# One expert-output copy a chunk earlier, warm-up products around the first gather, and head work moved between VectorE and GpSimd

## Chip, cores and metric

The kernel runs on one core of one Trainium2 chip. The metric is the device time of one execution in microseconds (us), lower is better. Float32 arithmetic is emulated on TensorE: each product of two float32 matrices is computed as three products of "high" and "low" parts in the fp32r format.

## What is computed

Two transformer blocks in a row over 256 tokens of width 1024. The first block has two layers with a second stream of 256 context tokens beside the tokens `x`; each layer norms both streams, projects them (`h @ w_in`), norms the query and key heads, rotates the heads of `x` by position (rope), attends, mixes, and runs a SwiGLU. The second block has an even layer (differential attention, a Mamba scan, SwiGLU) and an odd layer (sparse attention "nsa", latent attention "mla", then a mixture of 8 experts with two chosen per token). What the change touches, cut from the reference:

```python
qa, ka = apply_rope(qa, cos, sin), apply_rope(ka, cos, sin)      # x heads, first block
qc, kc = apply_rope(qc, cos, sin), apply_rope(kc, cos, sin)
qac = rms_norm(qac, q_norm)                                      # context heads, no rope
...
q = apply_rope(rms_norm(q, nsa_q_gain), cos, sin)                # odd layer, 8 heads of 64
...
logits = t @ router
top_val, top_idx = lax.top_k(logits, 2)
for e in range(8):
    out = out + gates[:, e:e + 1] * swiglu(t, w_gate[e], w_up[e], w_down[e])
```

## The kernel before

The program is a row of blocks; between two blocks all engines meet. Within a block each engine has its own instruction list, written out by hand, and executes it in that order; semaphores connect them. SP's queue issues the weight loads into a ring of four slots (`load_stream`, and the `sync` list of `moe`).

**A weight chunk's way.** In `linear`, `ffn` and `moe` a piece of weights (128x1024 float32) lands in the ring; ScalarE copies it to its high part `w_hi` (L978 in `linear`, L1188 in `ffn`, L3335 and L3340 in `moe`), VectorE subtracts that from the piece to get `w_lo` (L1066, L1262, L3407), TensorE multiplies (L880 to L882: high by high, low by high, high by low). Only three buffer pairs exist in `linear`, so the split of piece q waits until TensorE is through with piece q-3.

**Linear over the context (first block).** `linear` starts with a front: TensorE turns the normed rows, ScalarE makes `src_hi` (L690), VectorE `src_lo` (L646), eight tiles of 128x256. VectorE's order is: `w_lo` of piece 0, `src_lo` tiles 0 to 3, `w_lo` of piece 1, `src_lo` tiles 4 to 7, `w_lo` 2, `w_lo` 3, and so on. Piece 1 multiplies tiles 2 and 3, piece 2 tiles 4 and 5. Beside this GpSimd runs `x_turns1` (L1485): `rope_rows` (L529; L537 to L540) of the first eight heads of `x`, then the root of the context heads' mean squares (`rsqrts`, L494, the power on L500), for which it waits for VectorE, then `rope_rows` of the second eight heads. The context heads are squared, summed, scaled and multiplied with their gain on VectorE (`ctx_heads1`, L1496) after chunk 1 and chunk 2. This block runs twice: with 6 chunks in layer 0, where other small weight loads ("riders") are interleaved on the same SP queue, and with 3 chunks in layer 1.

**Linear of the odd layer.** Seven chunks. GpSimd runs `nsa_heads` (L2255): after the first eviction it norms eight query heads alone (`norm_rows`, L503, with squares on L510, five halving additions on L514, the power on L518, scale L523, gain L526), then waits for VectorE's mean squares of the keys and takes their root (L500), then ropes the queries. VectorE runs `nsa_keys` (L2270): squares of two key pairs after chunk 3, then key 0 after chunk 4 and key 1 after chunk 5 (scale L1462, gain L1469, rope L537 to L540). The last evictions (L1095) are of chunks 5 and 6. After its last product TensorE runs warm-up products (`tail=14`).

**The experts.** `moe` (L3122) walks through jobs b (8 in this trace), each of `FC` = 22 steps r. At step r TensorE does `up` of chunk r (12 products of 512 columns), on even steps it turns the activation of the pair before (L3249), and on odd steps it does `down` of two earlier chunks (L3249's result, split into `act_hi`, L3353, and `act_lo`, L3428). So a job's last two downs happen at step 1 of the next job. The job's output in banks 0 and 1 is then copied: `keep_output` on ScalarE (`y_hi`, L3324, two halves, and the turned pick matrix, L3326) and `keep_output_rest` on VectorE (`y_lo`, L3398). Both are called at step 3: ScalarE's behind that step's weight splits and `act_hi`, VectorE's behind the splits of gate and up but ahead of those of down and of `act_lo`. TensorE's `down` at step 3 writes the same banks and waits for `y_kept`.

Before the walk, `moe` makes the first pick matrices on VectorE (L3377), TensorE gathers the tokens in four parts (L3218), ScalarE and VectorE split them (L3315, L3384), and then the first weights are split. `keep_warm(p, pe, bank, n)` (L262) issues n products of 128 columns on TensorE whose result nobody reads.

Of the kernel before, what the change touches and what calls it, by code (L numbers as in the profile page):

```python
# [23 lines left out]
NT = T // P  # L24
D = 1024
KT = D // P
HD = 64
# [466 lines left out]
def rsqrts(p, pool, widths, parts=P, first=0):  # L494

    for w in widths:
        p.roots += 1
        pool.wait_ge(p.meansq.sem, p.roots)
        v = p.small[0:parts, first:first + w]
        pool.tensor_tensor(v, v, p.neg_half[0:parts, 0:w], ALU.pow).then_inc(p.rstd.sem, 1)  # L500
# [984 lines left out]
def x_turns1(p, proj, queries):  # L1485

    def beside(pool, taken):
        for a in (0, 896):
            rope_rows(pool_chain(p, pool), pool, heads_of(proj, a, 8), p.con_at(CON1, "rope_c", NT),
                      p.con_at(CON1, "rope_s", NT), p.big[:, 0:2048])  # L1490
            if a == 0:
                rsqrts(p, pool, [16 if queries else 4])
    return beside


# [759 lines left out]
def nsa_heads(p):  # L2255

    def beside(pool, taken):
        chain, junk = pool_chain(p, pool), p.big[:, 0:2048]
        pool.wait_ge(*taken(1))
        v = heads_of(p.proj, 0, 8)  # L2260
        norm_rows(p, chain, pool, v, [(0, 8, p.row(ROWS2, "nsa_q"))], junk, True)
        rsqrts(p, pool, [8])
        rope_rows(chain, pool, v, p.con_at(CON2, "rope_c", NT), p.con_at(CON2, "rope_s", NT), junk)
    return beside


# [3 lines left out]
def nsa_keys(p):  # L2270

    keys = [heads_of(p.proj, 768 + 256 * w, 2) for w in range(2)]
    st = p.small[:, 0:8]

    def inline(dve, chain, c):
        if c == 3:
            for w in range(2):
                square_sums(p, chain, dve, keys[w], p.work[:, 0:256], st[:, 4 * w:4 * w + 4])
            mean_squares(p, dve, st, HD)
        if c == 4:  # L2280
            rsqrt(p, dve, st)
        if c in (4, 5):
            for w in (c - 4,):
                scale_heads(chain, dve, keys[w], st[:, 4 * w:4 * w + 4])
                gain_heads(chain, dve, keys[w], p.row(ROWS2, "nsa_k", 1 + w, HD))
                rope_rows(chain, dve, keys[w], p.con_at(CON2, "rope_c", NT), p.con_at(CON2, "rope_s", NT), p.work[:, 512:1024])
    return inline
# [834 lines left out]
def moe(p):  # L3122
# [63 lines left out]
    with nc.Block(no_gpsimd_drain=True) as block:  # L3186
# [20 lines left out]
        def _(pe):  # L3207
# [69 lines left out]
            def step(i, b, r, first, last):  # L3277
# [21 lines left out]
                if r == FC + 2:  # L3299
                    turn_weights(i, b)  # L3300
                    for q in range(4):
                        scatter(i, b, q)

            for part in range(4):
                gather(0, 0, part)
            walk(pe, between, step)

        @block.scalar
        def _(act):
            between = act.value_load(p.trip[0:1, 1:2], min_val=1, max_val=3)  # L3310

            def keep_job(i, j, part):

                act.wait_ge(*job_at(gathered, i, 2, 2 * j + part + 1))
                act.activation(sources[j // 2 % 2][0][:, 2 * part:2 * part + 2, :].rearrange("p k s -> p (k s)"),  # L3315
                               p.ps[G_BANK[part]][:, :], ACT.Copy).then_inc(job_hi.sem, 1)

            def keep_output(i, j):

                act.wait_ge(*at(p.w_used[DOWN], i, (j + 1) * FC))  # L3320
                if not (isinstance(i, int) and j == 0):
                    act.wait_ge(*job_at(scattered, i, 4, 4 * j))
                for hf in range(2):
                    act.activation(yH[:, hf * 512:hf * 512 + 512], p.ps[hf][:, :], ACT.Copy).then_inc(y_hi.sem, 1)  # L3324
                act.wait_ge(*job_at(wt_turned, i, 1, j + 1))
                act.activation(WT, p.ps[5][:, 0:T], ACT.Copy).then_inc(wt_kept.sem, 1)  # L3326

            def step(i, b, r, first, last):
                k = b * FC + r

                def hi_side(half):
                    if half == 0:
                        act.wait_ge(*loaded_at(p.slot_loaded, g0, i, k))
                    act.wait_ge(*at(p.w_used[half], i, k - 1))
                    act.activation(sets[k % 2][0][:, half, :], side_piece(k, half), ACT.Copy).then_inc(p.w_hi[half].sem, 1)  # L3335

                def hi_down(m):
                    act.wait_ge(*loaded_at(p.dn_loaded, 0, i, m))
                    act.wait_ge(*at(p.w_used[DOWN], i, m - 1))
                    act.activation(sets[m % 2][0][:, DOWN, :], down_piece(m), ACT.Copy).then_inc(p.w_hi[DOWN].sem, 1)  # L3340

                if r < FC:
                    hi_side(0)
                    hi_side(1)
                c = k // 2 - 1
                if r % 2 == 0 and there(r, 2, first):
                    act.wait_ge(*at(p.w_used[1], i, 2 * c + 2))
                    act.activation(th[:, c % 2, :], p.ps[2 + c % 2][:, 0:T], ACT.Tanh, scale=0.5).then_inc(th_ready.sem, 1)
                if r % 2 and there(r, 3, first):
                    hi_down(k - 3)  # L3350
                    act.wait_ge(*pair_at(a_turned, i, c + 1))
                    act.wait_ge(*at(p.w_used[DOWN], i, 2 * c))
                    act.activation(p.actH[:, :], p.ps[4][:, 0:T], ACT.Copy).then_inc(act_hi.sem, 1)  # L3353
                    hi_down(k - 2)
                if r == 3 and not first:
                    keep_output(i, b - 1)
                if r - 3 in GATHER_AT and b % 2 and not last:
                    keep_job(i, b + 1, GATHER_AT.index(r - 3))
                if r == FC + 2:
                    keep_output(i, b)  # L3360

            for part in range(4):
                keep_job(0, 0, part)
            walk(act, between, step)

        @block.vector
        def _(dve):
# [33 lines left out]
            def step(i, b, r, first, last):  # L3401
                k = b * FC + r

                def lo(m, piece, kind):
                    wh, wl = [v[:, kind, :] for v in sets[m % 2]]
                    dve.wait_ge(*at(p.w_hi[kind], i, m + 1))
                    dve.tensor_tensor(wl, piece, wh.bitcast(F32), ALU.subtract).then_inc(p.w_lo[kind].sem, 1)  # L3407

                if r < FC:
                    lo(k, side_piece(k, 0), 0)  # L3410
                    lo(k, side_piece(k, 1), 1)
                if r == 3 and not first:
                    keep_output_rest(i, b - 1)
                c = k // 2 - 1
                bank = p.ps[2 + c % 2]
                if r % 2 == 0 and there(r, 2, first):
                    dve.wait_ge(*pair_at(th_ready, i, c + 1))
                    dve.scalar_tensor_tensor(out=zz[:, c % 2, :], in0=th[:, c % 2, :], scalar=1.0, in1=bank[:, 0:T],
                                             op0=ALU.add, op1=ALU.mult).then_inc(half_ready.sem, 1)
                    dve.wait_ge(*pair_at(half_ready, i, c + 1))  # L3420
                    if not (first and r < 6):
                        dve.wait_ge(*pair_at(a_turned, i, c - 1))
                    dve.scalar_tensor_tensor(out=aJ[:, c % 2, :], in0=zz[:, c % 2, :], scalar=0.5, in1=bank[:, T:2 * T],
                                             op0=ALU.mult, op1=ALU.mult).then_inc(a_ready.sem, 1)
                if r % 2 and there(r, 3, first):
                    lo(k - 3, down_piece(k - 3), DOWN)
                    dve.wait_ge(*pair_at(act_hi, i, c + 1))
                    dve.tensor_tensor(p.actL[:, :], p.ps[4][:, 0:T], p.actH[:, :].bitcast(F32),  # L3428
                                      ALU.subtract).then_inc(act_ready.sem, 1)
                    lo(k - 2, down_piece(k - 2), DOWN)  # L3430
                if r - 3 in SCATTER_AT and not first:
                    add_scattered(i, b - 1, SCATTER_AT.index(r - 3))
                if r == 6 and b % 2 and not last:
                    dve.wait_ge(*job_at(wt_turned, i, 1, b))
                    make_pick(i, b + 1)
                if r - 4 in GATHER_AT and b % 2 and not last:
                    keep_rest(i, b + 1, GATHER_AT.index(r - 4))
                if r == FC + 2:
                    keep_output_rest(i, b)
                    for q in range(4):  # L3440
                        add_scattered(i, b, q)
# [195 lines left out]
```

## Time and profile before

| what | value |
|---|---|
| median of 3 runs | 2532.47 us (2528.02 to 2534.73) |
| the profiled execution's own time | 2531.21 us |
| span of the profiled execution | 2529.0 us |
| TensorE busy | 2367.0 us, 94% |
| VectorE busy | 1764.6 us, 70% |
| ScalarE busy | 1262.2 us, 50% |
| GpSimd busy | 186.8 us, 7% |
| moved by DMA | 542.42 MB, mean 214 GB/s |

Names in the profile: PE is TensorE's matrix product, PEld its weight load, DVE is VectorE, ACT ScalarE, POOL GpSimd, SP the queue that issues loads. A row of a timeline gives start, duration, engine, line, operation, output and inputs, the count of merged instructions, and in brackets how long the engine had been idle and what ended that. The TensorE clock column is the granted clock as a share of 2.4 GHz. "PEq" of a line means the engine sequencer, in practice the meeting of all engines between two blocks. A start and a duration are on the engine: an instruction that is held up by something shows a longer duration.

### The profile page before, as it was taken

Reading aid. Unit: us, or ns where it says so; the run is one execution under the profiler, and the core shown is the slowest. Engines: PE = TensorE matmul, PEld = TensorE weight load, DVE = VectorE, ACT = ScalarE, POOL = GpSimd, SP = SyncE. Lnnn points to the kernel's source line nnn. Section 1 sums busy time; section 2 is a strip of 40 time slices with the busy share of each in tenths; the row PEclk is TensorE's granted clock in tenths of the full one; section 3 lists DMA queues with packets and bytes.
Section 4 is the critical chain, followed back from the end, with each engine's and each line's share of the span. In section 5 each row is a group of like instructions: output and inputs, shape, how many; then the busy total and the mean of one; then the engine's idle time right before and its main releaser. Section 6 shows DMA issues by size and latency. Waiting matters only on the chain. (4 is left out here: it accounts for less than half of the span.)

```text
span 2529.0 us, 37705 instructions
## 1 busy us (share of the span) xinstructions
PE 2367.0 (94%) x14147; PEld 1996.9 (79%) x14147; DVE 1764.6 (70%) x2539; ACT 1262.2 (50%) x1891; POOL 186.8 (7%) x168
## 2 busy tenths in 40 slices
PE   7889999999998999999799998879999999999998
PEld 6677689889986779988689987567787877877876
DVE  3555565565567565567765567558999999998997
ACT  2245244344443544442444442336777777776775
POOL 0310000000005000008100013000000000000000
PEclk9889999999999999999999997799999999999999
DMA  8520565646644055534045551027998988998995
GB/s 322 232 105 34 200 241 221 230 175 225 222 154 150 1 189 191 184 133 163 1 169 181 187 209 43 1 92 299 352 352 323 370 343 332 360 338 334 352 346 220
DMA packets 82199, 542.42 MB, mean 214 GB/s; under 512 B 9328, under 2 KB 9840, under 8 KB 33904
## 3 DMA queue, kind: packets, MB, share of 16 engines
q1 hardware_dynamic: 79184, 529.57, 56.2%
q10 hardware_dynamic: 2848, 10.55, 1.1%
q8 instruction: 114, 1.87, 0.3%
q14 instruction: 53, 0.43, 0.1%
HBM read 539.03 MB, written 1.05 MB: 214 GB/s over the span
## 5 line engine op out<-in xcount | busy, mean ns | idle before, releaser
L3407 DVE TENSOR_TENSOR w_lo<-ring,w_hi 128x1024 fp32r<-128x1024 f32 x528 | 617.8, 1219 | 28.2 <-ACT w_hi L3340 25.4
L880 PE MATMUL bank<-w_hi,src_hi 128*128 128x512 f32 (+1 forms) x1184 | 477.3, 403 | 20.8 <-DVE src_lo L646 12.7
L881 PE MATMUL bank<-w_lo,src_hi 128*128 128x512 f32 (+1 forms) x1184 | 464.9, 393 | 0.0
L882 PE MATMUL bank<-w_hi,src_lo 128*128 128x512 f32 (+1 forms) x1184 | 464.3, 392 | 0.0
L880 PE MATMUL bank<-src_hi,w_hi 128*128 128x256 f32 x1472 | 422.9, 287 | 7.9 <-DVE src_lo L646 7.3
L1188 ACT ACTIVATE w_hi<-ring 128x1024 fp32r<-128x1024 f32 x260 | 274.2, 1057 | 297.4 <-PE bank L882 273.2
L1262 DVE TENSOR_TENSOR w_lo<-ring,w_hi 128x1024 fp32r<-128x1024 f32 x260 | 317.9, 1223 | 146.9 <-ACT w_hi L1188 146.3
L881 PE MATMUL bank<-src_lo,w_hi 128*128 128x256 f32 x1472 | 417.2, 283 | 0.0
L882 PE MATMUL bank<-src_hi,w_lo 128*128 128x256 f32 x1472 | 417.1, 283 | 0.0
L3335 ACT ACTIVATE w_hi<-ring 128x1024 fp32r<-128x1024 f32 x352 | 352.5, 1055 | 2.0 <-PE bank L882 2.0
L880 PEld LDWEIGHTS bank<-src_hi,w_hi 128*128 128x128 f32 x1472 | 282.6, 192 | 21.0 <-issue 15.7
L880 PEld LDWEIGHTS bank<-w_hi,src_hi 128*128 128x128 f32 x1184 | 225.0, 190 | 78.8 <-issue 29.1
L880 PE MATMUL bank<-w_hi,act_hi 128*128 128x512 f32 x688 | 271.9, 395 | 15.2 <-DVE act_lo L3428 15.2
L881 PEld LDWEIGHTS bank<-src_lo,w_hi 128*128 128x128 f32 x1472 | 282.9, 192 | 2.3 <-issue 0.7
L882 PEld LDWEIGHTS bank<-src_hi,w_lo 128*128 128x128 f32 x1472 | 282.9, 192 | 0.0
L881 PE MATMUL bank<-w_lo,act_hi 128*128 128x512 f32 x688 | 271.2, 394 | 0.0
L882 PE MATMUL bank<-w_hi,act_lo 128*128 128x512 f32 x688 | 270.1, 393 | 0.0
L882 PEld LDWEIGHTS bank<-w_hi,src_lo 128*128 128x128 f32 x1184 | 224.9, 190 | 50.4
L881 PEld LDWEIGHTS bank<-w_lo,src_hi 128*128 128x128 f32 x1184 | 225.7, 191 | 44.4 <-issue 0.7
L978 ACT ACTIVATE w_hi<-ring 128x1024 fp32r<-128x1024 f32 x120 | 126.5, 1060 | 228.8 <-PE bank L882 145.4
L1066 DVE TENSOR_TENSOR w_lo<-ring,w_hi 128x1024 fp32r<-128x1024 f32 x120 | 171.9, 1439 | 84.1 <-ACT w_hi L978 83.6
L3340 ACT ACTIVATE w_hi<-ring 128x1024 fp32r<-128x1024 f32 x176 | 185.3, 1053 | 2.9 <-PE bank L882 2.9
(439 smaller groups left out, 2771.0 us busy)
## 6 DMA issues: line engine op xcount, KB each, us to landing
ring<-in_moe SPq DMA_DIRECT2D x176, 1024.0 KB, 6.7
ring<-in_ffn SPq DMA_DIRECT2D x66, 1536.0 KB, 6.7
ring<-in_moe SPq DMA_DIRECT2D x176, 512.0 KB, 5.7
ring<-in_ffn_ev SPq DMA_DIRECT2D x22, 1536.0 KB, 6.6
oT<-in_w_ada SPq DMA_DIRECT2D x20, 1024.0 KB, 6.9
big<-in_w_ada SPq DMA_DIRECT2D x20, 1024.0 KB, 8.4
ring<-in_w_in SPq DMA_DIRECT2D x18, 1024.0 KB, 7.9
ring<-in_w_out SPq DMA_DIRECT2D x12, 1024.0 KB, 9.9
```

The costliest lines, as they stand in the source:

```text
L880: pe.matmul(out, ah, bh, start=start and i == 0, stop=False, skip_group_check=True)
L881: pe.matmul(out, ah, bl, start=False, stop=False, skip_group_check=True)
L882: mm = pe.matmul(out, al, bh, start=False, stop=stop and i == n - 1, skip_group_check=True)
L978: act.activation(p.wH[:, b, :], p.ring[:, g % RING, (q % 2) * PIECE:(q % 2 + 1) * PIECE], ACT.Copy).then_inc(p.w_hi[b].sem, 1)
L1066: ins = dve.tensor_tensor(p.wL[:, b, :], p.ring[:, g % RING, (q % 2) * PIECE:(q % 2 + 1) * PIECE], p.wH[:, b, :].bitcast(F32), ALU.subtract)
L1188: act.activation(p.wH[:, kind, :], piece(c, kind), ACT.Copy).then_inc(p.w_hi[kind].sem, 1)
L1262: dve.tensor_tensor(p.wL[:, kind, :], piece(c, kind), p.wH[:, kind, :].bitcast(F32), ALU.subtract).then_inc(p.w_lo[kind].sem, 1)
L3335: act.activation(sets[k % 2][0][:, half, :], side_piece(k, half), ACT.Copy).then_inc(p.w_hi[half].sem, 1)
L3340: act.activation(sets[m % 2][0][:, DOWN, :], down_piece(m), ACT.Copy).then_inc(p.w_hi[DOWN].sem, 1)
L3407: dve.tensor_tensor(wl, piece, wh.bitcast(F32), ALU.subtract).then_inc(p.w_lo[kind].sem, 1)
```

## The change

Four edits; no arithmetic of the result changes, only where and when it is done.

1. `moe`: `keep_output` and `keep_output_rest` are called at step 2 in place of step 3. On ScalarE the call stands behind step 2's tanh; on VectorE it stands behind step 2's two activation operations.
2. `moe`: ten warm-up products before the first gather and ten after it.
3. `x_turns1` (both context linears): GpSimd ropes both groups of eight heads first and takes the context's root afterwards.
4. Odd layer's linear: the squares, sums and mean squares of the eight query heads go from GpSimd to VectorE (after chunk 1); GpSimd takes the root (now over 16 values by `rsqrts`), scales, applies gain and rope, and takes the keys' root last. VectorE turns key 0 after chunk 5 and key 1 after chunk 6, in place of after 4 and 5.

```diff
@@ x_turns1
         for a in (0, 896):
             rope_rows(pool_chain(p, pool), pool, heads_of(proj, a, 8), p.con_at(CON1, "rope_c", NT),
                       p.con_at(CON1, "rope_s", NT), p.big[:, 0:2048])
-            if a == 0:
-                rsqrts(p, pool, [16 if queries else 4])
+        rsqrts(p, pool, [16 if queries else 4])
@@ nsa_heads
-        pool.wait_ge(*taken(1))
         v = heads_of(p.proj, 0, 8)
-        norm_rows(p, chain, pool, v, [(0, 8, p.row(ROWS2, "nsa_q"))], junk, True)
+        st = p.small[:, 224:240]
+        rsqrts(p, pool, [16], first=224)
+        pool.wait_ge(p.rstd.sem, p.roots)
+        scale_heads(chain, pool, v, st)
+        gain_heads(chain, pool, v, p.row(ROWS2, "nsa_q"))
+        rope_rows(chain, pool, v, p.con_at(CON2, "rope_c", NT), p.con_at(CON2, "rope_s", NT), junk)
         rsqrts(p, pool, [8])
-        rope_rows(chain, pool, v, p.con_at(CON2, "rope_c", NT), p.con_at(CON2, "rope_s", NT), junk)
@@ nsa_keys, inline(dve, chain, c)
+        if c == 1:
+            square_sums(p, chain, dve, heads_of(p.proj, 0, 8), p.work[:, 0:1024], p.small[:, 224:240])
+            mean_squares(p, dve, p.small[:, 224:240], HD)
+            p.meansq.passed(1)
+            p.rstd.passed(1)
...
-        if c == 4:
+        if c == 5:
             rsqrt(p, dve, st)
-        if c in (4, 5):
-            for w in (c - 4,):
+        if c in (5, 6):
+            for w in (c - 5,):
@@ moe, TensorE
+            keep_warm(p, pe, p.ps[4], 10)
             for part in range(4):
                 gather(0, 0, part)
+            keep_warm(p, pe, p.ps[4], 10)
             walk(pe, between, step)
@@ moe, ScalarE, step
-                if r == 3 and not first:
+                if r == 2 and not first:
                     keep_output(i, b - 1)
@@ moe, VectorE, step
                     lo(k, side_piece(k, 1), 1)
-                if r == 3 and not first:
-                    keep_output_rest(i, b - 1)
...
                     dve.scalar_tensor_tensor(out=aJ[:, c % 2, :], in0=zz[:, c % 2, :], scalar=0.5, in1=bank[:, T:2 * T],
                                              op0=ALU.mult, op1=ALU.mult).then_inc(a_ready.sem, 1)
+                if r == 2 and not first:
+                    keep_output_rest(i, b - 1)
```

## Rows read from the trace of the kernel before

**Rows 1.** Busy time by stretch: from, to, length, engines, granted clock, DMA.

```profile
1717.00:2529.00 812.00, 787.80 (x3520) 637.25 (x3520) 742.15 (x863) 575.05 (x738) 0.00 (x0) 0.99 0.89 337
```

**Rows 2.** Waits, TensorE, 1725 to 2510 us: waiter, releaser, total, times, longest.

```profile
PE bank L880 <- DVE act_lo L3428: 14.0, 7, 2.2
```

**Rows 3.** Timeline of TensorE at one change of job (steps 1 to 3).

```profile
1818.12 0.39 PE L882 MATMUL bank<-w_hi,act_lo 128*128 128x512 f32 x1
...
1821.48 0.48 PE L880 MATMUL bank<-w_hi,src_hi 128*128 128x512 f32 x1
...
1826.47 0.47 PE L880 MATMUL bank<-w_hi,act_hi 128*128 128x512 f32 x1 [1.93 <-DVE act_lo L3428]
```

**Rows 4.** Timeline of ScalarE at the same change of job.

```profile
1816.36 2.00 ACT L3335 ACTIVATE w_hi<-ring 128x1024 fp32r<-128x1024 f32 x2
...
1822.99 1.07 ACT L3324 ACTIVATE y_hi<-bank 128x512 fp32r<-128x512 f32 x2
...
1824.21 2.02 ACT L3335 ACTIVATE w_hi<-ring 128x1024 fp32r<-128x1024 f32 x2
```

**Rows 5.** Timeline of VectorE at the same change of job.

```profile
1818.54 2.35 DVE L3407 TENSOR_TENSOR w_lo<-ring,w_hi 128x1024 fp32r<-128x1024 f32 x2
1823.61 1.29 DVE L3398 TENSOR_TENSOR y_lo<-bank,y_hi 128x512 fp32r<-128x512 f32 x2 [2.72 <-ACT y_hi L3324]
```

**Rows 6.** Timeline of TensorE from the router to the first expert.

```profile
1700.73 3.37 PE L265 MATMUL bank<-ident 128*128 128x128 f32 x28
1707.24 0.58 PE L3218 MATMUL bank<-pick,xn_hi 128*128 128x256 f32 x1 [3.14 <-DVE pick L3377]
...
1713.76 0.28 PE L3218 MATMUL bank<-pick,xn_lo 128*128 128x256 f32 x1
1717.02 0.76 PE L880 MATMUL bank<-w_hi,src_hi 128*128 128x512 f32 x1 [2.98 <-DVE w_lo L3407]
```

**Rows 7.** Busy time and granted clock (third figure from the end) by microsecond, there.

```profile
1706.00:1707.00 1.00, 0.00 (x0) 0.00 (x0) 0.69 (x4) 0.00 (x0) 0.00 (x0) 0.80 0.00 0
...
1720.00:1721.00 1.00, 1.00 (x5) 0.77 (x5) 0.28 (x1) 0.99 (x1) 0.00 (x0) 0.88 0.79 311
```

**Rows 8.** Front of layer 1's context linear, timelines of GpSimd, VectorE, TensorE.

```profile
798.82 2.45 POOL L540 TENSOR_TENSOR proj<-big 128x1024 f32<-128x1024 f32 x1
...
797.03 5.19 DVE L646 TENSOR_TENSOR src_lo<-work,src_hi 128x256 fp32r<-128x256 f32 x4
...
803.50 1.43 DVE L646 TENSOR_TENSOR src_lo<-work,src_hi 128x256 fp32r<-128x256 f32 x4
804.85 2.35 DVE L1066 TENSOR_TENSOR w_lo<-ring,w_hi 128x1024 fp32r<-128x1024 f32 x2
...
806.26 0.40 PE L880 MATMUL bank<-w_hi,src_hi 128*128 128x512 f32 x1
```

**Rows 9.** End of that linear, timelines of VectorE and TensorE.

```profile
820.72 2.48 DVE L1469 TENSOR_TENSOR projc<-projc,rows 128x256 f32<-128x256 f32 x1
...
823.80 0.66 PE L1593 MATMUL bank<-ident,projc 128*128 128x128 f32 x2 [5.78 <-PEq L954]
```

**Rows 10.** Layer 0's context linear, timelines of ScalarE and TensorE.

```profile
125.53 2.01 ACT L978 ACTIVATE w_hi<-ring 128x1024 fp32r<-128x1024 f32 x2 [9.70 <-DMA ring<-in_w_in]
...
131.78 1.05 PE L339 MATMUL bank<-small,rows 128*128 128x2 f32 x8 [3.76 <-DVE rows L331]
...
142.02 1.07 PE L323 MATMUL bank<-oT,rows 128*32 128x256 f32 x16 [2.02 <-DVE mod L349]
```

**Rows 11.** Odd layer's linear, timelines of GpSimd, VectorE, TensorE.

```profile
1509.08 5.97 POOL L514 TENSOR_TENSOR big<-big 128x512 f32<-128x512 f32 x5
...
1515.71 2.91 POOL L518 TENSOR_TENSOR small<-small,neg_half 128x16 f32<-128x16 f32 x1
...
1515.89 1.22 DVE L1066 TENSOR_TENSOR w_lo<-ring,w_hi 128x1024 fp32r<-128x1024 f32 x1 [1.35 <-ACT w_hi L978]
...
1541.84 1.94 PE L2371 MATMUL bank<-ident,proj 128*128 128x128 f32 x8 [5.33 <-PEq L954]
```

## The prediction

> **What bounds the kernel now.** I read the page's busy shares first, then the stretch of the experts, then who waits there, then the timelines of single places. TensorE is busy 2367.0 of 2529.0 us, 94%, so only its gaps and its slow-clock stretches can be won. The experts take 812 us, TensorE busy for 787.8 of them and VectorE for 742.2 [rows 1]: TensorE leads, VectorE has about a tenth to spare. The list of waits shows that TensorE stops there almost only at the seven changes of job: 14.0 us in 7 waits on `act_lo`, 2.0 each [rows 2]. The rest of the change lies in three linears and at the start of the experts, where VectorE and GpSimd decide.
>
> **Part 1, output copied at step 2.** Before, TensorE ends step 3's `up` and cannot go on with `down` until 1826.47 [rows 3]: `act_lo` stands on VectorE behind `y_lo`, and VectorE sat idle 2.72 us for `y_hi`, which ScalarE started only at 1822.99 [rows 4, 5]. Afterwards ScalarE reaches the copy with nothing else to do but to wait for the job's last `down`. That ends at 1818.12 + 0.39 = 1818.5 [rows 3]. From the start of `y_hi` to the next weight split it takes 1824.21 - 1822.99 = 1.22 [rows 4]. So step 3's first weight split, which ran at 1816.36, starts at 1819.8, 3.4 us later, and is queued behind this wait; it is done at 1820.8, the second at 1821.8, the `down` split at 1822.9, `act_hi` at about 1823.2. VectorE does `y_lo` in 1.29 by 1820.5, then step 3's first `w_lo` from 1820.9 to 1822.1 (1.17 each, half of 2.35 [rows 5]). TensorE wants it at 1821.48 [rows 3]: a new wait of 0.65. The rest of VectorE's list ends with `act_lo` at about 1824.9, and `up` ends at 1825.1. `down` starts there in place of 1826.47: 1.4 us won. Seven changes of job: **-9.8 us**. The unknown is how much of the 3.4 us on ScalarE reaches TensorE; ends: none (the whole 2.0 is won, -14) and all (3.4 - 2.0 = 1.4 lost each, +10). I take the value worked out from the lead that the rows show: `w_lo` was done at 1819.7, 1.8 ahead of its use. ScalarE and VectorE are back at their old times or earlier from step 4 on, so nothing is late next. SP's loads wait for `w_lo`, which moves by at most 2.4 us, and no engine waited for a load in the experts.
>
> **Part 2, warm-up products.** Fourteen such calls left 28 records in 3.37 us [rows 6], so ten cost 2.4 us at full clock. TensorE is idle 3.14 us before the gather and 2.98 before the first `up` [rows 6]; the second ten fit in that gap, the first ten overrun it by about 1.4 us (the block starts about 1 us before the gather does). What they may give: the gather ran from 1707.24 to 1714.0, 6.8 us at the 1.2 GHz level; the mean grant of 0.80 in the microsecond from 1706 puts the first fall at 1706.6; at the first `up` the clock was low again, until about 1720.2 (0.88 in that microsecond) [rows 7]. At 2.4 GHz the 32 gather products would take some 3.8 us, and the 3.2 us of low clock before 1720.2 would give back some 1.4. If the first ten come in time: +1.4 - 3.0 = -1.6 for the gather (the splits follow it), and -1.4 for the first `up`: -2.9. If the clock has fallen when they start, they cost about 4.5 us themselves, the gather ends later by up to 2.5, and only the second saving stands: +1. The start of the block and the fall of the clock are within 0.3 us of each other, so I take the middle: **-1.5 us**.
>
> **Part 3, both ropes first.** Two sides. At the end: in layer 1 the second rope holds VectorE's last gain for 2.48 us where the same form needs 0.43 elsewhere, and the block ends at 823.8 after a TensorE gap of 5.78 [rows 9]. Without it VectorE's last three operations end 3.4 us earlier. In layer 0 it stands behind the two TensorE gaps of [rows 10], 3.76 and 2.02.
>
> At the front: the second rope now starts at 801.3, in the stretch where TensorE waits for VectorE operation by operation. The rows show what a rope does there. While GpSimd's last two rope operations ran (until 801.27), four `src_lo` took 5.19 us; the next four, with GpSimd silent, took 1.43 [rows 8]. The starts and ends fit strict turns: one VectorE operation, one GpSimd operation. Going on in turns, the four operations of the second rope (about 1.15, 1.15, 2.25 and 2.2 of their own) push `src_lo` 2 to 4.5, `w_lo` 1 by 4.7 and `w_lo` 2 by 6.7 us. TensorE had started on that piece at 806.26, 0.1 us after `w_lo` was ready [rows 8]: no slack. So TensorE is 6.5 us late by then. Layer 1: +6.5 - 3.4 = **+3**. Its ends: -3.4 (front free) and +6 (the new gap also brings the clock down once). Layer 0: the same +6.7 at the front, and it is passed on, since SP issues the last weight chunks behind the riders, which wait for TensorE, and ScalarE waited for that chunk until 125.53 [rows 10]. Against it the gaps of 3.76 and 2.0 shrink by some 3.9, and the slow clock after each (about 1.6 us a time) may go. **+1**, ends -3.9 and +6.
>
> **Part 4, odd layer's linear.** GpSimd loses the squares and additions: 1.9 + 6.0 (five additions 5.97 [rows 11]). VectorE gains a square and a reduction of 128x1024, each taken at the 1.22 of an operation of that size [rows 11], and a small one, after chunk 1, where it was waiting for ScalarE; `w_lo` of the next piece comes 0.3 us later, three ahead of its use. GpSimd ends at about 1531 and not 1536, so the keys' operations on VectorE, held there as the gain was in [rows 9], are free: a whole key then takes 2.2. VectorE's tail behind TensorE's last product (about 1533.8, 0.8 later than before since `w_lo` 12 and 13 now meet the rope): eviction 0.76, key 1 in 2.2, end 1537.4 in place of 1541.3: -3.9. TensorE's gap of 5.33 at 1541.84 [rows 11] shrinks to 0.8, so the next block may begin at full clock: -1. **-5**, ends -1 and -9 (the fast clock holds on through the small products).
>
> A row and a page differ here. The power over 16 values ran from 1515.71 to 1518.62, and a `w_lo` that began 0.2 us into it took its plain 1.22 [rows 11]. The Trainium skill, "SBUF — State Buffer", Who interferes with whom, says that a VectorE instruction with two SBUF inputs and a GpSimd instruction that reads SBUF exclude one another for the whole instruction. For the ropes the trace agrees (5.19 against 1.43); for the power it doesn't, and I go by the row.
>
> **Sum.** -9.8 - 1.5 + 3 + 1 - 5 = -12.3. Against the profiled execution's own 2531.2 this gives 2518.9; the median of the runs is 1.3 higher, so 2520.
>
> **Rivals.**
> 1. *The front takes no harm* (VectorE gets in between, or the pieces have lead I don't see). Then part 3 gives -3.4 - 3.9 in place of +4: 2520 - 11.3 = 2508.7. For it: VectorE is only 70% busy. Against: 5.19 against 1.43. Chance 0.08.
> 2. *The stall at the change of job only changes its name*: `w_lo` of step 3 or of `down` comes late by 2.0 and takes the place of `act_lo`. Part 1 is 0: 2530. For it: ScalarE's 3.4 us delay is larger than the 2.0 won. Against: the lead of 1.8. Chance 0.10.
> 3. *Slower: ScalarE's in-order wait for the last `down` reaches TensorE whole.* Place: step 3's first `up`, seven times. Price 3.4 - 2.0 = 1.4 each, +9.8 in place of -9.8: 2539.6. It decides once the delay that reaches TensorE is over 2.0, that is if the lead of 1.8 is really below 0.4 after VectorE's own delay of 2.4. Chance 0.05.
> 4. *The power holds VectorE too*: in the odd layer it would now start near 1511.7, hold `w_lo` 8 until 1514.6, done 1515.8, where TensorE wants it at 1514.8: +1, 2521. That is what the page's rule gives. Chance 0.10.
>
> **Numbers.** The forecast has 0.67; its own range, with the ends above partly taken, is 2513 to 2526. The measurement tells 0.3% (7.6 us) from no change, so faster means below 2524.9. Faster: 0.62 of the forecast, 0.08, 0.09 of rival 4: 0.79. Same: 0.05, 0.10, 0.01, 0.01: 0.17. Slower: 0.04 of rival 3. The range goes from 2510 to 2529, leaving out rival 1, rival 3 and part of rival 2.
>
> **What would show it.** Part 1: at each change of job `y_hi` starts 0.1 us after the last `down`; TensorE waits about 0.65 us for `w_lo` and `down` starts 1.4 earlier. No such wait and 2.0 won would make me too cautious; one of 2 us or more makes rival 2 or 3. Part 2: gather in under 4.5 us, and 0.23 us apart from the first `up` on. Part 3: six or more us of TensorE gaps within the first ten of both context linears, none at the end. A front without them makes the prediction wrong by 11 us. Part 4: GpSimd's rope ends before 1532, and the next block starts near 1538 on the old scale.

## The result, and the profile after

The changed kernel takes 2512.66 us in the median of 5 runs (2507.91 to 2520.87), against 2532.47 before (also the median of five, where the table above has three): 19.8 us less, ratio 0.993 with an interval of 0.9911 to 0.995. The forecast was 2520 with 2510 to 2529. The profiled execution took 2507.91 us with a span of 2506.1, 22.9 less than that of before; it is 4.8 us below its own median and that of before 1.3 below, so about 3 us of these 22.9 are luck.

The table cuts both spans at the starts of blocks (first instruction of GpSimd or TensorE in them; "experts" begins at the first `up`). In brackets: us at the 1.2 GHz level, worked out from the granted clock. "nsa, mla and output linear" is called the nsa and mla block below.

| stretch, us | before | after | difference |
|---|---|---|---|
| up to layer 0's context linear | 92.6 (14.2) | 91.3 (10.8) | -1.3 |
| that linear | 61.2 (13.4) | 60.9 (13.2) | -0.3 |
| from there to layer 1's | 639.1 (24.7) | 639.4 (25.0) | +0.3 |
| layer 1's context linear | 30.8 (10.4) | 33.9 (15.9) | +3.1 |
| attention behind it | 90.6 (9.0) | 87.6 (0.0) | -3.0 |
| to the root in the odd linear's front | 573.0 (10.2) | 571.7 (10.2) | -1.3 |
| odd layer's linear from there | 54.4 (2.5) | 51.7 (0.0) | -2.7 |
| nsa, mla and output linear | 151.9 (62.4) | 149.1 (54.6) | -2.8 |
| router and gather | 23.3 (7.0) | 23.0 (3.4) | -0.3 |
| experts | 812.0 (13.3) | 797.4 (8.9) | -14.6 |

The waits of TensorE from 1712 to 2480 us, the experts: waiter, releaser, total, times, longest. It answers to [rows 2].

```profile
PE bank L880 <- DVE w_lo L3416: 3.6, 7, 0.5
```

The 14.0 us on `act_lo` are gone; seven waits of 0.5 on step 3's first `w_lo` have come, where 0.65 was forecast. One change of job in the timelines of TensorE, ScalarE and VectorE, beside [rows 3 to 5]:

```profile
1812.34 0.50 PE L880 MATMUL bank<-w_hi,src_hi 128*128 128x512 f32 x1 [0.44 <-DVE w_lo L3416]
...
1808.73 1.09 ACT L3333 ACTIVATE y_hi<-bank 128x512 fp32r<-128x512 f32 x2 [2.08 <-PE bank L882]
...
1809.96 2.02 ACT L3344 ACTIVATE w_hi<-ring 128x1024 fp32r<-128x1024 f32 x2
...
1809.36 1.29 DVE L3407 TENSOR_TENSOR y_lo<-bank,y_hi 128x512 fp32r<-128x512 f32 x2 [0.57 <-ACT y_hi L3333]
1811.06 3.50 DVE L3416 TENSOR_TENSOR w_lo<-ring,w_hi 128x1024 fp32r<-128x1024 f32 x3 [0.41 <-ACT w_hi L3344]
```

ScalarE idles 2.08 us for the last `down`, and the step's weight splits stand behind that. The front of layer 1's context linear, in the timelines of GpSimd, VectorE and TensorE, beside [rows 8, 9]:

```profile
802.80 2.52 POOL L539 TENSOR_TENSOR big<-proj,con 128x1024 f32<-128x1024 f32 x1
805.40 3.25 POOL L540 TENSOR_TENSOR proj<-big 128x1024 f32<-128x1024 f32 x1
...
795.74 7.38 DVE L646 TENSOR_TENSOR src_lo<-work,src_hi 128x256 fp32r<-128x256 f32 x4
803.04 3.35 DVE L1066 TENSOR_TENSOR w_lo<-ring,w_hi 128x1024 fp32r<-128x1024 f32 x1
806.55 3.39 DVE L646 TENSOR_TENSOR src_lo<-work,src_hi 128x256 fp32r<-128x256 f32 x4
...
824.53 0.42 DVE L1469 TENSOR_TENSOR projc<-projc,rows 128x256 f32<-128x256 f32 x1
...
806.46 0.79 PE L880 MATMUL bank<-w_hi,src_hi 128*128 128x512 f32 x1 [4.27 <-DVE w_lo L1066]
...
825.55 0.41 PE L1592 MATMUL bank<-ident,projc 128*128 128x128 f32 x2 [2.40 <-PEq L954]
```

Four `src_lo` now take 7.38 us (5.19 before) and the next `w_lo` 3.35 in place of 1.21: the two engines take turns until the second rope is over. TensorE waits 4.27 us for that `w_lo`, and starts piece 1 at the low clock (0.79 for the product behind the gap, where the one at 1812.34 above has 0.50 at full clock). At the end the gain runs at its own 0.42 (2.48 in [rows 9]), and the gap before the next block has shrunk from 5.78 to 2.40.

The odd layer's linear, timelines of GpSimd, VectorE and TensorE, beside [rows 11]:

```profile
1509.28 3.81 POOL L500 TENSOR_TENSOR small<-small,neg_half 128x16 f32<-128x16 f32 x1 [23.72 <-DVE small L1456]
...
1509.11 1.22 DVE L1066 TENSOR_TENSOR w_lo<-ring,w_hi 128x1024 fp32r<-128x1024 f32 x1
1510.58 1.23 DVE L1066 TENSOR_TENSOR w_lo<-ring,w_hi 128x1024 fp32r<-128x1024 f32 x1 [0.26 <-ACT w_hi L978]
...
1522.87 1.77 DVE L1456 TENSOR_SCALAR small<-small 128x8 f32<-128x8 f32 x1
1524.55 4.57 DVE L1066 TENSOR_TENSOR w_lo<-ring,w_hi 128x1024 fp32r<-128x1024 f32 x2
...
1525.82 0.39 PE L880 MATMUL bank<-w_hi,src_hi 128*128 128x256 f32 x1 [2.36 <-DVE w_lo L1066]
...
1536.55 1.06 PE L2378 MATMUL bank<-ident,proj 128*128 128x128 f32 x8 [0.74 <-PEq L954]
```

The gap before the next block is 0.74 and not 5.33. But the rope now meets the last two pieces, and TensorE waits 2.36 us for `w_lo` 12.

The start of the experts, timeline of TensorE, beside [rows 6]:

```profile
1697.86 4.13 PE L265 MATMUL bank<-ident 128*128 128x128 f32 x20 [1.85 <-PEq L3047]
...
1705.56 2.39 PE L265 MATMUL bank<-ident 128*128 128x128 f32 x20
1708.70 0.47 PE L880 MATMUL bank<-w_hi,src_hi 128*128 128x512 f32 x1 [0.75 <-DVE w_lo L3416]
```

The first ten warm-up calls take 4.13 us: the clock falls 0.6 us after they start, at 1698.44, and is back at 1701.85. The second ten run at full clock and take 2.39.

### The profile page after: what moved, and what is told of

It is laid out like the page before. It is cut to its first block and busy times, and to the rows that moved or that the text cites. A ratio compares the mean times of both kernels' runs of the same rounds, so it can differ in the third digit from the quotient of the medians.

```text
span 2506.1 us, 37778 instructions
## 1 busy us (share of the span) xinstructions
PE 2359.8 (94%) x14187; PEld 1993.8 (80%) x14187; DVE 1766.1 (70%) x2542; ACT 1261.8 (50%) x1891; POOL 181.5 (7%) x160
## 5 line engine op out<-in xcount | busy, mean ns | idle before, releaser
L3416 DVE TENSOR_TENSOR w_lo<-ring,w_hi 128x1024 fp32r<-128x1024 f32 x528 | 616.8, 1218 | 29.5 <-ACT w_hi L3349 24.7
L880 PE MATMUL bank<-w_hi,src_hi 128*128 128x512 f32 (+1 forms) x1184 | 478.0, 404 | 32.0 <-DVE src_lo L646 12.7
## 6 DMA issues: line engine op xcount, KB each, us to landing
ring<-in_w_out SPq DMA_DIRECT2D x12, 1024.0 KB, 10.5
```

Source lines behind the costliest of these rows:

```text
L880: pe.matmul(out, ah, bh, start=start and i == 0, stop=False, skip_group_check=True)
```

## The experiments

Each part of the change was first undone alone. The experiments ran on three chips, each beside the kernel before (median 2528.42 us for the first four, 2531.92 for the next four, 2529.41 for the last three). So whole times are compared by their ratio to it, which is 0.993 for the changed kernel; 0.001 is 2.5 us.

**The copy back at step 3.**

```diff
-                if r == 2 and not first:
+                if r == 3 and not first:
                     keep_output(i, b - 1)
```

(and VectorE's part likewise)

> The changed kernel with the output copied at step 3 again, as before. My theory: the waits of 0.5 us on the first w_lo at each change of job become waits of 2.0 us on act_lo, seven times, +10.4 us between the first up and the end; and with waits of 2 us the low clock stretches of about 3.4 us that the kernel before had at 1928 and 2331 us come back in some of them (1 to 2 us lost each), so +11 to +14 in all, 2524 to 2527 us against the changed kernel's 2512.7. Rival (the clock has nothing to do with the waits at the changes of job): no low clock between the first up and the last job, and +10.4 alone. Rival 2 (the gain in the experts was not from the copy): under +5.

Measured: 2527.21 us median (2517.8 to 2546.16), ratio to before 1.0001 (0.9977 to 1.0025). By the two ratios the kernel is 18 us slower than the changed one, give or take some 8. The experts take 811.8 us, 14.4 more than in the changed kernel. The waits of TensorE in the experts, and the busy time and granted clock around one change of job:

```profile
PE bank L880 <- DVE act_lo L3437: 14.0, 7, 2.2
```

```profile
1927.00:1928.00 1.00, 0.00 (x0) 0.00 (x0) 1.00 (x2) 1.00 (x2) 0.00 (x0) 1.00 0.00 0
...
1929.00:1930.00 1.00, 1.00 (x3) 0.79 (x3) 1.00 (x2) 1.00 (x2) 0.00 (x0) 0.50 0.76 119
1930.00:1931.00 1.00, 1.00 (x4) 0.73 (x3) 1.00 (x2) 0.42 (x1) 0.00 (x0) 0.50 0.97 397
1931.00:1932.00 1.00, 1.00 (x4) 0.81 (x3) 1.00 (x2) 0.77 (x1) 0.00 (x0) 0.50 1.04 434
1932.00:1933.00 1.00, 1.00 (x5) 0.78 (x5) 0.97 (x3) 0.29 (x1) 0.00 (x0) 0.90 1.03 418
```

The theory holds: behind three of the seven waits, those at 1825, 1928 and 2229, the clock is low for 3.4 us each. The time from one job's last `down` to the next job's shows the price. Where the clock stays up, it is 1.4 to 1.6 us longer than in the changed kernel (four times), where it falls 2.9 to 3.0 longer (three times). So the waits cost 7 x 1.5 = 10.4 and the three low stretches some 1.5 each, 4.4. Less about 0.4, which the changed kernel loses at its very end, where its own clock is low from 2497 us on, this makes the 14.4. The kernel before has two such stretches, at 1928 and 2331; in the changed kernel and in the profiles of all ten other experiments, with waits of 0.5 or none, there is none from 1725 to 2480 us.

**No warm-up products.** Both `keep_warm` lines left out in `moe`.

> The changed kernel without the twenty warm-up products. My theory: the gather runs at the 1.2 GHz level again and takes 6.6 us or more (4.1 now), the first 8 products of the first up are 0.43 apart and not 0.23; from the start of the block to the first up the time is about the same (warm-up products before the gather cost what the faster gather gives back: 0.2 us in all), so the whole costs 1.5 to 2 us, nearly all after the first up. Rival (the warm-up products gave the 3 us I had as the best case): +3 or more, half of it before the first up.

Measured: 2510.7 us median (2501.74 to 2525.64), ratio 0.9943 (0.9919 to 0.9967) against 0.993 with them, with intervals that overlap. The experts take 797.1. From the router's last four count products to the end of the twelfth product of the first `up`: 20.38 us, against 19.34 in the changed kernel. The same stretch is 19.34 to 20.24 in eight profiles with the warm-up products and 21.06 in the kernel before. So about 1 us by the profiles, nothing that the times show; more on it below. Two of my signs did not come: the gather took 5.6 us and not 6.6, and the first `up` ran at full clock.

**The root between the ropes again.**

```diff
+            if a == 0:
+                rsqrts(p, pool, [16 if queries else 4])
-        rsqrts(p, pool, [16 if queries else 4])
```

> The changed kernel with the context's root between the two ropes again. My theory: the front of both context linears loses its TensorE gap of 4 us on the first w_lo; layer 1's linear from block start to block start goes from 33.9 back to 30.8 us (-3.1), layer 0's from 60.9 to about 61.2. Against it the attention block after layer 1's linear starts at low clock again, because TensorE then idles 5.8 us before it and not 2.4, and takes about 4 us longer. In sum 0 to +2 us. Rival (the attention's 4 us were chance, not tied to that gap): -3 in sum and an attention as long as the changed kernel's.

Measured: 2513.78 us median (2506.27 to 2522.0), ratio 0.9931 (0.9908 to 0.9955), where the changed kernel has 0.993: the whole times show no difference. Layer 1's linear is 32.1 us, layer 0's 61.2. The early ropes thus cost 1.8 us in layer 1 in this pair and 3.1 against before (the linear is 33.7 to 34.6 in five profiles with them), and in layer 0 about nothing. The attention was 89.5 us, but it was 89.2 and 89.1 in the two experiments above, which have the early ropes and the short gap, with 7.2 us of low clock each, and 89.9 with the short gap in a later one. So my second claim, on the attention, fell: its 3 us can't be tied to the gap in front of it. Over all profiles it took 90.6 and 89.5 us with the long gap and 87.6 to 89.9 with the short one.

**The odd layer's linear as before.** `nsa_heads` and `nsa_keys` taken back.

> The changed kernel with the odd layer's linear as before (GpSimd norms the queries alone, keys turned after chunks 4 and 5). My theory: from GpSimd's small root of that block (L500) to the next block's start 54.4 us as before in place of 51.7 (+2.7), with a TensorE gap of 5.3 us before the next block, which then starts at the 1.2 GHz level and takes 2.8 us longer; +5.5 in sum. Rival (the next block's clock is not tied to that gap): +2.7 only.

Measured: 2516.28 us median (2513.38 to 2521.63), ratio 0.9955 (0.9939 to 0.997). The stretch is 54.4 us, as forecast, against 51.7 to 52.4 in the profiles that have this part. The block behind took 155.7, but with the part in place it took anything from 149.1 to 158.8 (54.6 to 85.3 us at low clock), so its length decides nothing. Its front does. GpSimd's root over 15x2 values there, in this run, the kernel before and the changed kernel:

```profile
1562.45 0.69 POOL L500 TENSOR_TENSOR small<-small,neg_half 15x2 f32<-15x2 f32 x1 [11.14 <-DVE small L2592]
```

```profile
1569.74 0.69 POOL L500 TENSOR_TENSOR small<-small,neg_half 15x2 f32<-15x2 f32 x1 [11.09 <-DVE small L2593]
```

```profile
1561.62 0.69 POOL L500 TENSOR_TENSOR small<-small,neg_half 15x2 f32<-15x2 f32 x1 [11.06 <-DVE small L2600]
```

From the block's start (1534.49, 1541.84 and 1536.55) that is 27.9 or 28.0 us in the two profiles with the long TensorE gap, and 25.1 in the changed kernel; in all eleven profiles with the short gap it is 23.7 to 26.6. In the two, the clock is low for the first 25 us of the block, in the eleven for 13.7 to 20.5 us of its front. So the theory fits here, and my rival does not: the part is worth 2 to 2.7 us in its own block and 1.3 to 4.2 behind it. What the rest of the block then does with its clock hides that in the whole. The ratios differ by 6 us, with intervals that overlap.

**A second rope that starts later.** This and the following are edits of the changed kernel.

```diff
         for a in (0, 896):
+            if a:
+                pool.wait_ge(*p.w_lo[0](2))
```

> The changed kernel, but GpSimd starts the second rope only when VectorE has finished w_lo of the fourth piece (one added wait, nothing left out). If the price of the front is VectorE and GpSimd taking turns where TensorE waits for VectorE: no TensorE gap on the first w_lo in either context linear, src_lo and w_lo at their own 1.4 us for four and 1.2, the first eviction of layer 1 at 19.1 us after the block's start in place of 25.5, the block 6 us shorter, 27.5 to 28 us; layer 0's shorter by 3 to 6 us. If instead any early rope costs, wherever it stands (it just moves the hold to the next pieces): less than 3 us won in layer 1.

Measured: 2498.48 us median (2496.66 to 2508.67), ratio 0.9868 (0.9853 to 0.9883), by the ratios 16 us less than the changed kernel. Layer 1's linear takes 27.5 us (33.9 in the changed kernel, 30.8 before), layer 0's 57.4 (60.9). VectorE in layer 1's front:

```profile
798.78 1.43 DVE L646 TENSOR_TENSOR src_lo<-work,src_hi 128x256 fp32r<-128x256 f32 x4
800.13 2.35 DVE L1066 TENSOR_TENSOR w_lo<-ring,w_hi 128x1024 fp32r<-128x1024 f32 x2
802.91 2.10 DVE L1066 TENSOR_TENSOR w_lo<-ring,w_hi 128x1024 fp32r<-128x1024 f32 x1 [0.42 <-ACT w_hi L978]
```

`src_lo` and `w_lo` run at their own times, and the rope's turns fall on the fifth and sixth piece (2.10 for 1.21), which have about 3 us of lead; TensorE has no wait on a `w_lo` there. The first eviction comes 19.2 us after the block's start. So it is the place of the rope that costs, not the rope. The two linears give 9.9 us; where the other 6 of the ratios come from, if they are real, no profile shows.

**Writes in place of the second rope.** The second group's rope is left out in both context linears; six constants of 128x1024 are written instead.

```diff
+                for m in range(6):
+                    pool_chain(p, pool)(pool.memset(p.big[:, 0:1024], 1.0))
```

> The changed kernel with the second group's rope left out of both context linears and, in its place, six writes of a constant to 128x1024 on GpSimd, which read nothing from SBUF. If GpSimd's reads are what holds VectorE: the six writes run beside src_lo and w_lo without stretching them (four src_lo from the first rope's end on at 0.36 us each, w_lo at 1.2), and TensorE has no 4 us gap on the first w_lo. If any GpSimd work holds VectorE: the same 3 to 4 us stretches as with the rope.

Measured, in one execution of 2509.35 us: layer 0's linear 54.2 us, layer 1's 27.8. Timelines of GpSimd and VectorE:

```profile
796.46 6.01 POOL L1494 MEMSET big<- 128x1024 f32 x6
...
797.27 1.21 DVE L1066 TENSOR_TENSOR w_lo<-ring,w_hi 128x1024 fp32r<-128x1024 f32 x1
798.64 1.43 DVE L646 TENSOR_TENSOR src_lo<-work,src_hi 128x256 fp32r<-128x256 f32 x4
799.99 2.35 DVE L1066 TENSOR_TENSOR w_lo<-ring,w_hi 128x1024 fp32r<-128x1024 f32 x2
```

Six writes in 6.01 us beside seven unstretched VectorE operations: it is the rope's reading of SBUF that holds VectorE. The Trainium skill, "SBUF — State Buffer", Who interferes with whom, says just this of a VectorE instruction with two SBUF inputs: it collides with a GpSimd instruction that reads, not with one that only writes. The trace agrees.

**The copy behind the side splits.**

```diff
                 if r < FC:
                     hi_side(0)
                     hi_side(1)
+                if r == 3 and not first:
+                    keep_output(i, b - 1)
...
-                if r == 2 and not first:
-                    keep_output(i, b - 1)
```

(VectorE's part at step 3 behind its two side splits, as in the kernel before)

> The changed kernel, with ScalarE's output copy at step 3 directly behind the step's two side splits, and VectorE's at step 3 behind its two side splits. Worked out from the rows: the side splits are no longer behind the wait for the last down, that wait is over when they end, act_lo is ready about 0.7 us before up ends. So my theory has no TensorE wait at the seven changes of job: 0.52 less each, -3.6 us in the experts. Rival (VectorE then does y_lo ahead of down's w_lo and act_lo and is late with them): a wait on act_lo or w_lo takes its place, no gain or a loss of up to 0.5 each.

Measured: 2503.64 us median (2498.02 to 2520.82), ratio 0.9904 (0.9873 to 0.9934). The list of TensorE's waits from 1711 to 2480 us is empty. ScalarE at a change of job:

```profile
1808.17 2.00 ACT L3344 ACTIVATE w_hi<-ring 128x1024 fp32r<-128x1024 f32 x2
1810.36 1.09 ACT L3333 ACTIVATE y_hi<-bank 128x512 fp32r<-128x512 f32 x2 [0.19 <-PE bank L882]
```

ScalarE waits 0.19 and not 2.08. The experts take 791.4 us, 6.0 less than in the changed kernel and 5.7 to 6.6 less than in the five other profiles with waits of 0.5 (797.1 to 798.0), although only 3.6 us of waits stood in the list. The rest is in the last section.

**Both.** The two edits together.

> The late second rope and the copy behind the side splits together. My theory: the two are in different blocks and add up, -6 (layer 1), -3 to -6 (layer 0) and -3.6 (experts), unless the attention behind a shorter linear starts at low clock and gives 4 back: 2495 to 2503 us. Rival (the front's price was hidden by the load that layer 0 waits for, and the clock gives back the rest): within 5 us of the changed kernel.

Measured: 2495.21 us median (2493.18 to 2503.78), ratio 0.9864 (0.9845 to 0.9882): 27.5, 57.2 and 791.3 us in the three stretches, so in the stretches they add up. The whole times don't show it: this is only 3.3 us below the late rope alone, and the ranges overlap.

**The same again, and two variants.**

> The kernel of the run before (late second rope, copy behind the side splits) once more, so that the next two are compared with it on the same chip: about 2495 us.

Measured: 2496.17 us median (2491.09 to 2505.99), ratio 0.9875 (0.9848 to 0.9902).

> The same kernel without the twenty warm-up products. From the profiles so far, the time from the router's last count product to the twelfth product of the first up is 19.3 to 20.2 us with them (seven executions) and 20.4 and 21.1 without. My theory: they are worth about 1 us and no more, so 20 to 21.5 us in that stretch and a median within 2 us of the other. Rival (they are worth the 3 us that I had as best case): 3 us or more in that stretch.

Measured: 2500.78 us median (2494.53 to 2517.57), ratio 0.9902 (0.9871 to 0.9934). The stretch took 18.95 us without the warm-up products and 19.33 with them. The medians are 4.6 apart the other way, with ranges that overlap. Neither is what I had expected. Over all profiles the stretch is 18.95, 20.38 and 21.06 without, 19.33 to 20.24 with. The 18.95 and the 21.06 have the same instructions; the clock fell for 3.4 us around the gather in the one and for 6.8 in the other. So 3 us show in no profile, and whether these products are worth anything stays open.

Layer 1's linear, with the instructions of the three before, took 28.8 us here and in the next one, in place of 27.5: the clock stayed low until 12.4 us after its start and not 9.2, and the first eviction came after 21.5 us.

For the last one only layer 0's linear differs: `if (a == 0) == queries:` in place of `if a:`, so there both ropes start late.

> The same kernel, but in layer 0's context linear both ropes start only when w_lo of the fourth piece is done (layer 1 as in the other: first rope at once, second late). If turn-taking is also what the first rope costs: the first four src_lo of layer 0's front take 1.4 and not 5.2 us, TensorE's first product waits 1 us and not 2.8, the linear is 2 to 4 us shorter than 57.3. Rival (the load of the fifth weight chunk decides layer 0's linear anyway, or two ropes late hold VectorE elsewhere): no change or longer.

Measured: 2496.29 us median (2493.03 to 2504.75), ratio 0.9874 (0.985 to 0.9899). VectorE and TensorE in layer 0's front:

```profile
97.58 1.42 DVE L646 TENSOR_TENSOR src_lo<-work,src_hi 128x256 fp32r<-128x256 f32 x4
...
98.14 0.47 PE L880 MATMUL bank<-w_hi,src_hi 128*128 128x512 f32 x1 [1.01 <-DVE src_lo L646]
```

The front is as free as expected (1.42 and 1.01), and the first eviction comes 23.4 us after the block's start, against 25.6 to 26.7 in the three before. But the linear took 54.5 us where the kernel without warm-up products, whose linear has the same instructions as the other, took 54.4. That one had 6.6 us of low clock; the other two took 56.8 and 57.2 with 10.5 and 13.7 us of it, this one has 10.2. So a gain of 2 us or so is possible and not shown; the kernel as a whole is not faster.

## Why the prediction was right, and where it fell short

The direction and the range held; the size did not quite: -12.3 forecast, -19.8 measured, with an interval of 12.7 to 22.5 less. By its own steps:

- **Part 1, -9.8.** The mechanism came out closely: a new wait of 0.65 forecast and 0.5 measured, on the piece named, with ScalarE's `y_hi` right behind the last `down` (0.05 us). The 7 x 1.5 = 10.4 of waits were real. What failed is the sum's silence about the clock: the 2 us waits at the changes of job also brought the clock down, twice in the profile before and three times with the copy undone. The seven spacings from one last `down` to the next shrank by 13.3 us from the kernel before, 10.4 of waits and 2.9 of two low stretches, and by 14.8 in the pair with three. So this one term is 3.5 to 5 of the missing 7.5.
- **Part 2, -1.5.** The profile shows the second of the two cases I had: the clock fell as the first ten ran (4.13 us), the gather took 4.1 us in place of 6.8, the two cancel. What was left is 1.5 us in the first `up`. This pair gives -1.7, the other profiles anything from a gain of 1 to a loss of 0.4: the -1.5 is not shown.
- **Part 3, +3 and +1.** Layer 1: +3.1. VectorE's turns with GpSimd were forecast operation by operation: `w_lo` 1 late by 4.7 (4.3 measured), the first eviction by 6.5 (6.4, from 19.1 to 25.5 us after the block's start). Layer 0: -0.3; the front's gap of 3.99 us and its low clock were paid back by the gaps that shrank (3.76 to 1.77, 2.02 to 0.30) and by two low stretches that vanished.
- **Part 4, -5.** -5.5 in this pair, but not as split. -2.7 in the block where -3.9 was forecast: the keys' mean squares ahead of `w_lo` 12 were held as well (1.77 for 0.17), TensorE waited 2.36 for it, and its last product came 1.9 us later than before and not 0.8. The next block won 2.8 us where -1 was forecast, all in its first 28 us: the low clock of 24.8 us there became 17.1.
- **Beyond the parts.** The stretches that the change touches, the front of the nsa and mla block among them, add up to -17.6. The other 5.3 of the profile's 22.9 are -3.0 in the attention, -1.3 each at the start and in the middle, and +0.3. No experiment ties them to the change, and some 3 us are the luck named above.

The rivals: the front did take harm (first rival out), the stall did not only change its name (second out), ScalarE's wait did not reach TensorE whole (third out). The fourth, the power holding VectorE, is out as well: with the power running until 1513.09 (recorded from 1509.28), the `w_lo` at 1510.58 took 1.23. Here the measurement differs from what the Trainium skill says of reading GpSimd instructions in "SBUF — State Buffer", Who interferes with whom.

## What to carry to other kernels

A wait that an in-order engine reaches early is not free: it holds everything queued behind it. Place an operation so that the engine arrives when the wait is just over (ScalarE 0.19 us before the last `down`, not 2.08), and put a second engine's SBUF-reading work where the first one has lead, not in a block's front: the same rope put a block's first eviction off by 6.4 us in one place and by nothing visible where it began later (19.2 us after the block's start in three profiles, against 19.1 before). When a stall goes, price the clock that fell behind it too, and compare stretches of the profile, since whole executions of one kernel here differ by 10 us and more in step with the clock. Cut a stretch short where the clock wanders: the front of a block told what its 150 us hid.

## What the runs showed that I had not expected

- **A TensorE wait costs more than its idle time.** Taking away seven waits of 0.52 us shortened the seven spacings from one last `down` to the next by 5.5 us, 0.79 each. Products start 0.23 us apart but are recorded with 0.40, so a gap's record leaves out 0.17; and the first product behind a gap is recorded with 0.50 in place of 0.39 or 0.40. 0.52 + 0.17 + 0.10 = 0.79, just that.
- **GpSimd's power over 16 values does not hold VectorE, but is itself held.** It took 3.81 us where a `w_lo` had begun 0.17 earlier, 2.91 or 2.92 in all six places of the kernel before, while the next `w_lo` ran through it unstretched.
- **The nsa and mla stretch spreads by 10 us with the same instructions** (149.1 to 158.8), in step with its time at the 1.2 GHz level (54.6 to 85.3 us). The gap in front of it decides some of that in the first 28 us; what decides the rest was not tried.
